# Odd mixer: query products before key/value products, weight units moved out of the attentions

## What is computed

```
def _mla_q(h, ...):    # rank 256, 16 heads of 64 + 32
    q = (rms_norm(h @ w_dq, q_norm_g) @ w_uq).reshape(b, t, 16, 96)
    return concat([q[..., :64], rope_2d(q[..., 64:], row, col)])
def _mla_kv(h, ...):   # rank 128, one shared rotated key part of 32
    ckv = h @ w_dkv
    c_kv, k_pe = ckv[..., :128], ckv[..., 128:]      # k_pe rotated on the latent tokens
    kv = (rms_norm(c_kv, kv_norm_g) @ w_ukv).reshape(b, t, 16, 64 + 64)
    return concat([kv[..., :64], k_pe for every head]), kv[..., 64:]
y_x = attention(q_x, [k_x, k_c], [v_x, v_c]) @ w_o
```

## Time and profile before

| | |
|---|---|
| median of three runs | 2368.94 us (2368.51 to 2370.61) |
| profiled execution | 2378.37 us, of which the span is 2376.6 us |
| TensorE, VectorE, ScalarE, GpSimd busy | 94%, 68%, 44%, 10% of the span |
| even attention, norm of the first item to first output product | 1436.7 to 1528.9 us |
| odd mixer's inputs, from the load freed by O_DQ to the first scores | 1986.8 to 2041.9 us |
| odd attention | 2041.9 to 2126.0 us |

### The profile page before, as it was taken

The page is one execution under the profiler, slowest core; times in us unless marked ns, Lnnn a source line. Parts: engine busy times, 40 slices in busy tenths (PEclk is TensorE's granted clock), DMA queues, the critical chain, the costliest instruction groups (busy, mean ns, idle before and its releaser), DMA issues. The chain is left out here.

```text
span 2376.6 us, 36004 instructions
## 1 busy us (share of the span) xinstructions
PE 2241.9 (94%) x15104; PEld 2044.0 (86%) x15104; DVE 1625.3 (68%) x2439; ACT 1048.6 (44%) x1512; POOL 238.6 (10%) x257
## 2 busy tenths in 40 slices
PE   6999998999999999999999998899999997697997
PEld 6999978999999997899998775698888875477997
DVE  5877886877887887887752567666455245656775
ACT  5443534443533443534453345435444224555663
POOL 2101222100210122210000005000000001000000
PEclk9999989999999998999998997999999998998999
DMA  5665524667466541666521112022222220103553
GB/s 210 237 213 195 202 74 177 230 218 264 164 228 226 189 165 54 231 234 239 184 84 64 54 54 77 1 72 107 97 99 91 105 89 36 53 20 119 182 178 107
DMA packets 48225, 333.84 MB, mean 140 GB/s; under 512 B 6012, under 2 KB 7132, under 8 KB 8768
## 3 DMA queue, kind: packets, MB, share of 16 engines
q1 hardware_dynamic: 37808, 268.45, 31.6%
q0 software_dynamic: 10256, 63.08, 7.4%
HBM read 330.46 MB, written 1.05 MB: 139 GB/s over the span
## 5 line engine op out<-in xcount | busy, mean ns | idle before, releaser
L1963 DVE TENSOR_TENSOR WLO<-RAW,WHI 128x2048 fp32r<-128x2048 f32 x252 | 586.3, 2328 | 272.5 <-ACT WHI L1417 269.8
L446 PE MATMUL PS<-XB,WHI 128*128 128x256 f32 (+1 forms) x3072 | 700.2, 323 | 15.9 <-DVE XB L2302 11.6
L1417 ACT CAST WHI<-RAW 128x2048 fp32r<-128x2048 f32 x252 | 480.3, 1909 | 322.9 <-DMA RAW<-in_dn_c 78.0
L446 PEld LDWEIGHTS PS<-XB,WHI 128*128 128x128 f32 x3072 | 516.8, 192 | 63.5 <-issue 19.1
L446 PE MATMUL PS<-XHI,WHI 128*128 128x272 f32 x1792 | 527.8, 297 | 17.8 <-ACT XHI L1424 15.0
L446 PE MATMUL PS<-XHI,WLO 128*128 128x272 f32 x1792 | 522.3, 294 | 0.0
L446 PE MATMUL PS<-XLO,WHI 128*128 128x272 f32 x1792 | 498.3, 292 | 0.0
L446 PE MATMUL PS<-XB,WLO 128*128 128x256 f32 (+1 forms) x1536 | 493.4, 321 | 0.0
L446 PEld LDWEIGHTS PS<-XHI,WHI 128*128 128x128 f32 x1792 | 346.4, 193 | 22.7 <-issue 18.5
L446 PEld LDWEIGHTS PS<-XHI,WLO 128*128 128x128 f32 x1792 | 345.9, 193 | 0.0
L446 PEld LDWEIGHTS PS<-XLO,WHI 128*128 128x128 f32 x1792 | 334.9, 193 | 0.5
(11 more groups left out here) (367 smaller groups left out, 2792.8 us busy)
## 6 DMA issues: line engine op xcount, KB each, us to landing
AW<-in_ada POOLq DMA_DIRECT2D x48, 1024.0 KB, 6.8
RAW<-in_up_a SPq DMA_DIRECT2D x44, 1024.0 KB, 5.0
RAW<-in_up_b SPq DMA_DIRECT2D x44, 1024.0 KB, 4.9
RAW<-in_up_c SPq DMA_DIRECT2D x44, 1024.0 KB, 4.8
RAW<-in_mix SPq DMA_DIRECT2D x30, 1024.0 KB, 4.9
RAW<-in_dn_a SPq DMA_DIRECT2D x22, 1024.0 KB, 4.9
RAW<-in_dn_b SPq DMA_DIRECT2D x22, 1024.0 KB, 4.9
RAW<-in_dn_c SPq DMA_DIRECT2D x22, 1024.0 KB, 4.8
```

The costliest lines, as they stand in the source:

```text
L446: return pe.matmul(o, w, x, start=first, stop=last)
L1417: act.copy(WHI1[:, s, :], RAW[:, s, :]).then_inc(w1_high, 1)
L1963: v.tensor_tensor(WLO1[:, s, :], RAW[:, s, :], WHI1[:, s, :].bitcast(F32), ALU.subtract)\
```

## The change

In `odd_inputs` the product of the squared query latent moves from behind O_DKV's context half into its middle, before the fifth of eight k steps; the query units come next, with the CKSQ and KPE products behind the first quarter; the key/value unit is second, and the pair swap of the queries stands behind its second key unit. Banks of PSUM are given out anew to fit, and the copies on ScalarE and the steps on VectorE follow the order of TensorE. The units in memory are reordered in the same way (query up before key/value up). The casts and subtractions of the output units leave both attentions: O_WO's cast goes behind the query copies, O_WO+1's behind the fourth key copy, O_WO+2's behind the second value copy, O_WO+3's behind the attention; the subtractions stand behind CKV (O_WO), behind the rotation (O_WO+1 and O_WO+2) and behind the attention. E_WOUT+2 and E_WOUT+3 move to the head of `even_output`.

```diff
-O_DQ, O_DKV, O_UKV, O_UQ, O_WO = ODD0, ODD0 + 1, ODD0 + 2, ODD0 + 3, ODD0 + 5
+O_DQ, O_DKV, O_UQ, O_UKV, O_WO = ODD0, ODD0 + 1, ODD0 + 2, ODD0 + 4, ODD0 + 5
...
-            elif O_UKV <= n < O_WO:
-                released.append((odd_done, 8 + 2 * (n - O_UKV)))
+            elif O_UQ <= n < O_WO:
+                released.append((odd_done, (2, 4, 12)[n - O_UQ]))
...
-                def dkv(z):
+                def dkv(z, inside=None):
                     split(O_DKV)
                     for k in range(CT):
+                        if inside is not None and k == CT // 2:
+                            inside()
...
+                def query_power():
+                    pe.wait_ge(odd_taken, 1)
+                    pe.wait_ge(norm_std[0], y_at(1))
+                    for t in range(2):
+                        last = mm(pe, PS[:, 2, 0:SEQ], ONES[:, 1, :], DQSQ[:, t, :], t == 0, t == 1)
+                    last.then_inc(odd_mm, 1)
...
-                dkv(0).then_inc(unit2_done, 1)
-
-                pe.wait_ge(tab_loaded, RT_LOADED)
-                pe.wait_ge(odd_taken, 1)
-                for t in range(2):
-                    last = mm(pe, PS[:, 3, 0:SEQ], ONES[:, 1, :], DQSQ[:, t, :], t == 0, t == 1)
-                last.then_inc(odd_mm, 1)
-                pe.wait_ge(odd_taken, 2)
-                mm(pe, PS[:, 0, :], ONES[:, 2, :], CKSQ[:, :], True, True).then_inc(odd_mm, 1)
-                mm(pe, PS[:, 1, 0:SEQ], PERM[:, :], KPE[:, CTX:L2], True, True).then_inc(odd_mm, 1)
+                dkv(0, query_power).then_inc(unit2_done, 1)
+
+                pe.wait_ge(odd_step, DQ_AT)
+                for n in range(4):
+                    u, b = O_UQ + n // 2, (6, 0, 4, 6)[n]
+                    pe.wait_ge(w1_loaded[slot_of[u]], 16 * loads[u])
+                    if n >= 2:
+                        pe.wait_ge(odd_taken, n)
+                    for j in range(3):
+                        for k in range(2):
+                            c = ((3 * n + j) % 6 * 2 + k) * P
+                            last = mm(pe, PS[:, b + j // 2, 256 * (j % 2):256 * (j % 2) + 256],
+                                      RAW[:, slot_of[u], c:c + P], DQ[:, k, :], k == 0, k == 1)
+                    last.then_inc(odd_done, 1)
+                    if n == 0:
+                        pe.wait_ge(odd_taken, 2)
+                        pe.wait_ge(norm_std[1], in_at(2))
+                        mm(pe, PS[:, 3, :], ONES[:, 2, :], CKSQ[:, :], True, True).then_inc(odd_mm, 1)
+                        pe.wait_ge(tab_loaded, RT_LOADED)
+                        pe.wait_ge(odd_std, 1)
+                        mm(pe, PS[:, 2, 0:SEQ], PERM[:, :], KPE[:, CTX:L2], True, True).then_inc(odd_mm, 1)
                 pe.wait_ge(w1_loaded[slot_of[O_UKV]], 16 * loads[O_UKV])
                 pe.wait_ge(odd_step, CKV_AT)
                 s = slot_of[O_UKV]
-                for n in range(4):
-                    if n >= 2:
-                        pe.wait_ge(odd_taken, 2 + n - 1)
+                for n in range(8):
+                    b = (4, 2, 6)[n % 3]
+                    pe.wait_ge(odd_taken, (5, 5, 6)[n] if n < 3 else 4 + n)
                     for j in range(2):
-                        last = mm(pe, PS[:, 4 + 2 * (n % 2) + j, :], RAW[:, s, (2 * n + j) * P:(2 * n + j + 1) * P],
-                                  CKV[:, :], True, True)
+                        if n < 4:
+                            last = mm(pe, PS[:, b + j, :], RAW[:, s, (2 * n + j) * P:(2 * n + j + 1) * P], CKV[:, :],
+                                      True, True)
+                        else:
+                            last = mm(pe, PS[:, b + j, :], CKV[:, (n - 4) * P:(n - 3) * P],
+                                      RAW[:, s, D + j * 512:D + (j + 1) * 512], True, True)
                     last.then_inc(odd_done, 1)
-                for n in range(4):
-                    pe.wait_ge(odd_taken, 2 + 4 + n - 1)
-                    for j in range(2):
-                        last = mm(pe, PS[:, 4 + 2 * (n % 2) + j, :], CKV[:, n * P:(n + 1) * P],
-                                  RAW[:, s, D + j * 512:D + (j + 1) * 512], True, True)
-                    last.then_inc(odd_done, 1)
-                pe.wait_ge(odd_step, DQ_AT)
-                for n in range(4):
-                    u = O_UQ + n // 2
-                    pe.wait_ge(w1_loaded[slot_of[u]], 16 * loads[u])
-                    pe.wait_ge(odd_taken, 2 + 8 + n - 1)
-                    for j in range(3):
-                        for k in range(2):
-                            c = ((3 * n + j) % 6 * 2 + k) * P
-                            last = mm(pe, PS[:, 4 + 2 * (n % 2) + j // 2, 256 * (j % 2):256 * (j % 2) + 256],
-                                      RAW[:, slot_of[u], c:c + P], DQ[:, k, :], k == 0, k == 1)
-                    last.then_inc(odd_done, 1)
+                    if n == 1:
+                        pe.wait_ge(odd_taken, 6)
+                        for t in range(4):
+                            last = mm(pe, PS[:, t // 2, 256 * (t % 2):256 * (t % 2) + 256], PERM[:, :], QR[:, t, :],
+                                      True, True)
+                        last.then_inc(odd_mm, 1)
                 pe.wait_ge(odd_taken, 2 + 12)
-                for t in range(4):
-                    last = mm(pe, PS[:, t // 2, 256 * (t % 2):256 * (t % 2) + 256], PERM[:, :], QR[:, t, :], True, True)
-                last.then_inc(odd_mm, 1)
                 pe.wait_ge(odd_step, ROTATED_AT)
...
                 act.wait_ge(pool2_step, HEADS_ZERO)
                 for n in range(4):
-                    b = 4 + 2 * (n % 2)
-                    act.wait_ge(odd_done, 8 + n + 1)
+                    b = (6, 0, 4, 6)[n]
+                    act.wait_ge(odd_done, n + 1)
                     act.copy(QR[:, n, :], PS[:, b + 1, 0:SEQ])
                     for odd in range(2):
                         q = slice(64 * odd, 64 * odd + 64)
                         last = act.copy(QH[q, 4 * n + odd:4 * n + 4:2, :], PS[q, b, :].rearrange("p (a b) -> p a b", a=2))
                     last.then_inc(odd_taken, 1)
+                high(O_WO)
+                for n in range(8):
+                    b = (4, 2, 6)[n % 3]
+                    act.wait_ge(odd_done, 4 + n + 1)
+                    if n < 4:
+                        for odd in range(2):
+                            q = slice(64 * odd, 64 * odd + 64)
+                            h = 4 * n % 8 + odd
+                            last = act.copy(KH[n // 2][q, h:h + 3:2, :], PS[q, b:b + 2, :])
+                    else:
+                        last = act.copy(VV[:, n - 4, :].rearrange("p (a b) -> p a b", a=2), PS[:, b:b + 2, :])
+                    last.then_inc(odd_taken, 1)
+                    if n in (3, 5):
+                        high(O_WO + n // 2)
...
-            def odd_weights(n):
-
-                if n in (1, 3, 5, 7):
-                    high(O_WO + n // 2)
-
-            softmax(ODD_ITEMS, len(EVEN_ITEMS), PR2, PTT2, (0, 1, 2, 3), odd_weights)
+            softmax(ODD_ITEMS, len(EVEN_ITEMS), PR2, PTT2, (0, 1, 2, 3), lambda n: None)
+            high(O_WO + 3)
...
+                rest(E_WOUT + 2)
+                rest(E_WOUT + 3)
...
+                v.wait_ge(odd_std, 2)
+                vs.did(v.reciprocal(CKSTD[:, :], CKSTD[:, :]))
                 v.wait_ge(odd_mm, OD_KPE)
-                od.did(v.tensor_tensor(SW[:, 0, :], PS[:, 1, 0:SEQ], RT[:, 1, :], ALU.mult))
+                od.did(v.tensor_tensor(SW[:, 0, :], PS[:, 2, 0:SEQ], RT[:, 1, :], ALU.mult))
                 od.link(v.tensor_tensor(KPE[:, CTX:L2], KPE[:, CTX:L2], RT[:, 0, :], ALU.mult))
                 od.did(v.tensor_tensor(KPE[:, CTX:L2], KPE[:, CTX:L2], SW[:, 0, :], ALU.add))
                 assert od.n == KPE_AT
-                v.wait_ge(odd_std, 2)
-                vs.link(v.reciprocal(CKSTD[:, :], CKSTD[:, :]))
+                vs.wait()
                 od.link(v.tensor_tensor(CKV[:, :], CKV[:, :], CKSTD[:, :], ALU.mult))
                 od.did(v.tensor_scalar(CKV[:, :], CKV[:, :], QNG[:, 2:3], None, ALU.mult))
                 assert od.n == CKV_AT
+                rest(O_WO)
...
+                rest(O_WO + 1)
+                rest(O_WO + 2)
```

More of the change, by code:

```diff
@@ L1781, in head_norm @@
                     act.copy(XB[:, :, 0, 4 + n - 6, :], two(G[:, 8 + n - 6, :])).then_inc(head_act, 1)
[L1782 to L1785, removed]
             def softmax(items, base, probs, turned, banks, between):
@@ L1821, in even_output @@
             def even_output():
+                high(E_WOUT + 2)
+                high(E_WOUT + 3)
                 for u in range(4):
@@ L1871, in odd_inputs @@
                 act.wait_ge(odd_mm, OD_DQ)
-                act.activation(DQSTD[:, :], PS[:, 3, 0:SEQ], ACT.Sqrt, bias=EPS6[:, 0:1]).then_inc(odd_std, 1)
+                act.activation(DQSTD[:, :], PS[:, 2, 0:SEQ], ACT.Sqrt, bias=EPS6[:, 0:1]).then_inc(odd_std, 1)
                 act.wait_ge(*released[O_DKV])
```

(19 more changed lines are left out.)

## The result

The changed kernel takes 2342.32 us (median of four runs, 2337.90 to 2343.44), the one before 2369.78 in the same comparison. The ratio is 0.9875, 95% interval 0.9861 to 0.9889. The two medians lie 27.5 us apart; the ratio, which is not formed from them, would be 29.6 us. The forecast was 26.1. Two more comparisons of the same pair gave 0.9887 (0.9872 to 0.9903) and 0.9886 (0.9871 to 0.9901).

The account below looks back on a forecast made before the run. TensorE was taken to bound the odd input products and attention, with a dependency chain between them. Savings of 16.0 + 8.0 + 2.1 = 26.1 us from 2368.94 gave 2342.8, forecast as 2343; range 2337 to 2351.

Parts of the forecast that it names:

- Query norm and query products first: Odd inputs: DQ ready 2.1 us sooner; key/value norm runs beneath query products, so the 5.91 us wait goes to nothing.
- ScalarE late next, 16 us saved: Odd inputs: ScalarE's copies and casts end last, covering the queries' rotation by 6.2 us; scores start 16 us sooner.
- Odd items, 8.0 us saved: Odd attention: without weight units the first 11 intervals take 2.217 us each, saving 8.0 us.
- Even items, 2.1 us and 0: Even attention: moving item 18's unit saves 2.1 us; moving item 4's saves 0, because TensorE paces that stretch.
- Rival 1: Even item 4's unit counts (2.2 us) or first odd scores meet warm TensorE (up to 1.7); 2339 us; chance 0.12.
- Rivals 2, 4 and 5: Key/value passes at lower clock, 2351 (0.06); attentions keep pace, 2353 (0.05); odd attention at lower clock, up to 2413 (0.02).
- Rival 3, GpSimd: Odd inputs: GpSimd's four key copies hold up VectorE, rotated queries 7.8 us later; 2344.5 us; chance 0.05.

Follow-up runs that it names:

- e5: The changed kernel with the product of the squared queries put back behind O_DKV's context half; 0.9901 of the kernel before.
- e1: The changed kernel with the four O_WO units back between the odd attention's items, new order kept; 0.9903 of the kernel before.
- e6: The changed kernel with casts and subtractions of O_WO+1 and O_WO+2 moved behind the odd attention; 0.9877 of the kernel before.
- e7: As e6, with O_WO's cast also moved from behind the fourth query quarter's copies to behind the second's; 0.9862 of the kernel before, repeated 0.9897.
- e2: The kernel before, its order kept, with only the odd units moved out from between the odd attention's items; 0.9951 of the kernel before.
- e3: The changed kernel with both E_WOUT units back in the even attention, behind items 4 and 18; 0.9900 of the kernel before.
- e4: The changed kernel with only E_WOUT+2 back behind item 4 of the even attention; 0.9878 of the kernel before.

## Why the prediction was right

*Query norm and query products first.* The forecast was that TensorE would wait 0.7 us for the squares and 0.6 for DQ, and that CKV would be ready 1.2 us before it is wanted. Measured: 0.57, 0.48 and 1.7. e5 shows that this chain is the one that counts.

*ScalarE late next, 16 us saved.* Measured 16.2, with 5.2 us of slack for the rotation (forecast 6.2). What I did not see in the prediction is how near TensorE is behind it: e1, e6 and e7 put TensorE's bound 2.6 us ahead of ScalarE's. It was no error of the sum, but it was the limit for anyone who would take more casts away. Nor did I see that up to 2.2 us of the old time there were the lower clock; the sum held without it, because it was built from the durations of the new chain and not from the waits that went away.

*Odd items, 8.0 us saved.* Right mechanism (e1 and e2, once each way), too small: 9.2. I let the first eleven intervals run at the later pace of 2.217 us; in the changed kernel the first two take 1.38 and 1.70, and that accounts for the 1.2 us. That these items start with scores made in advance (six passes ahead of the first norm) is my reading of the order; no run tested it.

*Even items, 2.1 us and 0.* Both right, by e3 and e4. At item 4 VectorE's 2.2 us lay beside the slow passes of TensorE. An engine can do visible extra work between two items and cost nothing, while the same work at item 18 costs all of its time.

*Rival 1, half of it.* The forecast gave this rival 0.12 and left its gain out of the sum. The first scores met the full clock in the profile: six passes in 2.84 us instead of 4.32, first norm 1.4 us sooner. With the 1.2 us of the items and 0.2 of the inputs this is the difference between the 28.9 us of the stages and the 26.1 forecast. That the medians, 27.5 us apart, came nearer to the forecast than the stages is luck, since whole times carry 3 us and more of noise. Behind the same gap of 2.56 us the six traces gave 3.09, 3.09, 3.08, 3.08, 3.62 and 4.70 us, so it is true mostly but not always. Behind 7.64 us it was 4.49 and 4.62, behind 1.10 us always 3.08 to 3.09. The other half (item 4) fell with e4.

*Rivals 2, 4 and 5* did not come: the key/value passes ran at 0.43 us, the items' pace changed, and the granted clock was 1.00 in the odd attention from 2021 to 2086.

*Rival 3, GpSimd.* The four key copies took 9.68 us instead of 7.75, with VectorE's subtraction beside them. GpSimd's fourth copy and the first step of the rotation on all of QR, in the changed kernel; then the subtraction and GpSimd's second copy in e7, where the subtraction starts just behind the first copy:

```profile
2002.41 3.83 POOL L667 COPY KH<-KPE 64x2048 f32<-64x2048 f32 x1
...
2005.74 1.58 DVE L2621 TENSOR_TENSOR QR<-QR,RT 128x1024 f32<-128x1024 f32 x1
```

```profile
1994.14 3.95 DVE L1968 TENSOR_TENSOR WLO<-RAW,WHI 128x2048 fp32r<-128x2048 f32 x1 [0.15 <-ACT WHI L1427]
...
1996.00 3.84 POOL L667 COPY KH<-KPE 64x2048 f32<-64x2048 f32 x1
```

Both engines held each other up, one instruction at a time. In the changed kernel the subtraction began while the third copy ran (2000.46 to 2002.35) and took 2.67 us instead of 2.29; the fourth copy began under the subtraction and took 3.83 instead of 1.89; the rotation's step began under the fourth copy and took 1.58 instead of 1.22. In e7 the subtraction took 3.95 us, the copy behind it 3.84, and the rotation's step, begun under the last copy, 2.34. In the kernel before, e1 and e2, where nothing of the kind lies beside them, every copy took 1.89 or 1.90 us and the step 1.22. The Trainium skill (SBUF, State Buffer: Who interferes with whom) has it that one of the two blocks the other for a whole instruction; the rows agree, in both directions, and each time it was the later of the two that grew. I had priced 1.9 us for VectorE; it lost 0.38 + 0.36 = 0.74 us, which is most of the missing 1.0 us of slack in the rotation, and GpSimd lost 1.94 us of the 11 us that it had.

## What to carry to other kernels

When a chain has two branches, start the one with the longer tail first, and lay the other's products and copies over that tail; then look at once for the engine that is now full, since here ScalarE ended the chain, only 2.6 us behind TensorE. Work placed "between" the items of a loop is free only where another engine sets the pace there; read the intervals of one instruction per item, with and without the extra work, summed over several items, because a late one can be made up by the next. For effects of 2 us in 2340, compare stages from an anchor inside the trace, not spans.

## What the runs showed of the hardware

The twelve profiles start the even attention anywhere between 1424.9 and 1436.7 us, though all that runs before is the same. TensorE's clock has a part in such differences at least where it could be read: the same six passes of the first scores took 2.84 us in the changed kernel, 4.54 in e3 and 4.30 in e5, each after the same pause of 2.56 us. The windows of both, the changed kernel and then e3 (whose window ends before the last two passes):

```profile
2017.50:2021.00 3.50, 2.84 (x6) 1.06 (x6) 2.68 (x7) 2.58 (x4) 0.00 (x0) 1.00 0.46 190
```

```profile
2018.00:2021.70 3.70, 3.14 (x4) 1.43 (x5) 1.85 (x3) 1.99 (x3) 0.00 (x0) 0.59 0.55 232
```

The granted clock is 1.00 in the first and 0.59 on average in the second; the two kernels have the same work from the even mixer's output on. In e3 even a pause of 1.69 us in the even attention was followed by 0.74. How much of the 12 us at the start is the clock was not taken apart.
